# Half of an output product moved into the attention ahead of it, and a bias table fetched in two parts

## The chip, the cores and the metric

The program runs on one core of one Trainium2 chip. The metric is the device time of one execution in microseconds (us); smaller is better.

## The reference

Two transformer blocks of depth 2 act on x of 512 tokens by 1024 channels, batch 1, in float32. The change touches the second block only. There, for each of two layers:

```python
proj = x @ w_in[l]                       # hq, hf, hi, hg | nq, kc, vc, ks, vs, kw, vw, gt
o_a = hgrn2_mixer(hq, hf, hi, hg, ...)   # 4 heads of 128: a gated linear recurrence
o_b = nsa_mixer(nq, kc, vc, ks, vs, kw, vw, gt, ..., rel_bias)   # 8 heads of 64
mix = concatenate([o_a, o_b]) @ w_out[l] # 1024 x 1024
x = layer_norm(ALPHA * x + mix, ...)
ffn = (silu(x @ w_gate[l]) * (x @ w_up[l])) @ w_down[l]
x = layer_norm(ALPHA * x + ffn, ...)
```

`hgrn2_mixer` is a recurrence whose output is scaled per head by its root mean square, then by silu of a gate. `nsa_mixer` is attention of three kinds for each head (compressed keys, selected blocks, a window), each with a causal mask, a bias by distance out of `rel_bias` and a softmax of its own; the three outputs are summed with gates.

## The kernel before, in words

The channels lie on the partitions: x is `xT`, 8 chunks of 128 channels by 512 tokens. Every large product is made of three matmuls for one (`product`, lines 251 to 253): operands are split into a high and a low part, and high x high, high x low and low x high are added in a PSUM bank. Weights come through a ring of two slots of 1024 columns (512 KB each). For each slot SyncE's queue loads (`load`), ScalarE makes the high part (`hi`, line 287), GpSimd subtracts for the low part (`lo`, line 295), TensorE multiplies and counts `slots_done`. Loads, `hi` and `lo` of slot n wait for slot n-2.

All engines have their instructions in an order written out by hand, and wait for each other on counting semaphores. In the second block a layer runs:

1. Input projections, then the recurrence `pe_hgrn` / `act_hgrn` / `dve_hgrn` / `pool_hgrn`: 16 units (4 heads of 4 token chunks). Decays fill banks 0 and 1 and are read by ScalarE (`dec_exp`), scores fill banks 2 and 3 and are masked by VectorE (`a_mask`), outputs of head h gather in bank 4 + h % 2 (`ho_ready`). The last six column tiles of the projection are made in halves between the first twelve units (`pe_turn`). For each head then: ScalarE squares (line 1704), TensorE forms the mean in bank 7 (`mean_square`, line 1639), ScalarE takes the root (lines 1713 and 1717), VectorE scales (`head_out`, line 1738, semaphore `hout`), GpSimd gates and splits (`gated`, lines 1790 to 1796, three steps of `hmix` per head). For the last head this stands at the very end.
2. The three-way attention `pe_nsa` / `dve_nsa` / `act_nsa`: 16 units, four pairs of heads (hp) by four query tiles (i); unit u has (i + 1) x 128 keys. `scores(u)` (line 1855) writes six maps, VectorE adds the bias from `tab2` and takes the minimum (line 1974), ScalarE exponentiates and sums (line 2008), VectorE normalises (`post`, lines 1932 to 1945), TensorE turns the probabilities through banks 5 and 6 (`turn`, line 1865, first the selected ones SLC, then the window WIN), ScalarE copies them back (`back`, line 1992). Once per pair the compressed map is turned (`turn_cmp`, line 1874, bank 7) and copied (`back_cmp`, line 1952), and the value product `pv` (lines 1885 and 1894) fills bank 7, which `take` splits (lines 1998 and 1956, semaphore `o_taken`). `tab2`, the whole bias table of 8 heads (2 MB), lies over the recurrence's operands and is loaded when the last recurrence unit is done (line 2087).
3. The output product `pe_out`: 8 column tiles m of 8 chunks, 24 matmuls each, alternately in banks 4 and 5, one weight slot per tile; `dve_sum` (line 2022) adds ALPHA x, `add_output` sums for the norm. Its chunks 0 to 3 are the recurrence's heads, 4 to 7 the attention's pairs.
4. Layer norm, feed-forward, layer norm.

The last lines of `pe_nsa` before, which set TensorE's order:

```python
scores(0)
scores(1)
for u in range(NU):
    if u + 2 < NU:
        scores(u + 2)
    turn(u, SLC)
    if u and u % NT == 0:
        pv(u // NT - 1)
    turn(u, WIN)
    if u % NT == NT - 1:
        turn_cmp(u // NT)
pv(NSA // 2 - 1)
```

## Time and profile before

| | |
|---|---|
| median of 3 runs | 3761.97 us (3760.66 to 3763.39) |
| profiled execution | 3766.26 us, span 3764.5 us |
| TensorE busy, mean granted clock | 3539.1 us (94%), 0.969 |
| VectorE, ScalarE, GpSimd busy | 1628.5, 1251.0, 1442.9 us |
| attention of the second block, first layer | 2378.8 to 2490.0 us |
| output product, first layer | 2490.0 to 2533.9 us |

A line of a timeline has start and duration in us, engine, line of the code, operation, output <- inputs, shapes and count of merged instructions; in brackets the idle time before it and what ended it. PE is TensorE, PEld its weight load, DVE VectorE, ACT ScalarE, POOL GpSimd, SPq SyncE's queue. A line of a windows view has from:to and length in us, then busy time (and instructions) of PE, PEld, DVE, ACT and POOL, then the granted clock of TensorE (1.00 is 2.4 GHz, 0.50 is 1.2), the share of the DMA engines and GB/s. Matmuls are pipelined, so the durations of successive ones overlap: the distance of two starts is the price of one. A plain f32 matmul shows as two instructions.

### The profile page before, as it was taken

To read this page: it belongs to the slowest core of one execution; us is meant where nothing else is said; L and a number is where in the kernel's file an instruction comes from. 1 tells how busy PE (TensorE), PEld (TensorE's weight loads), DVE (VectorE), ACT (ScalarE), POOL (GpSimd) and SP (SyncE) were. 2 spreads that over 40 slices of the span, in tenths; PEclk is the share of its full clock that TensorE was granted. 3 is DMA by queue.
4 is the path that set the end of the run, shared out by engine and by line. 5 is a ranking of instruction groups with operands and counts; after the bars stand their busy time and mean duration, and the time that the engine had idled before them with its cause. 6 is when DMAs were issued, how large, how long until landed. Compare 5 with 4: busy or idle time off the path is not lost. (4 is left out here: it accounts for less than half of the span.)

```text
span 3764.5 us, 45087 instructions
## 1 busy us (share of the span) xinstructions
PE 3539.1 (94%) x16148; PEld 2780.2 (74%) x16148; DVE 1628.5 (43%) x2540; ACT 1251.0 (33%) x2114; POOL 1442.9 (38%) x615
## 2 busy tenths in 40 slices
PE   7999899899989998998999899789999898899998
PEld 5888766688868887666888687467887676568886
DVE  5441354644244423456442429634321548533312
ACT  2222346322232223464222343543222433622222
POOL 3444321344434443222444335123445244024443
PEclk9999999999999999999999999899999998899999
DMA  4223311222323223211323321012223221013222
GB/s 150 97 94 97 106 62 34 76 97 94 97 73 100 95 97 105 68 40 62 100 95 97 118 79 34 34 46 75 97 95 97 100 69 46 1 57 100 95 94 91
DMA packets 85520, 307.10 MB, mean 82 GB/s; under 512 B 11109, under 2 KB 11749, under 8 KB 83854
## 3 DMA queue, kind: packets, MB, share of 16 engines
q1 hardware_dynamic: 85390, 305.38, 24.8%
q8 instruction: 80, 1.31, 0.2%
q14 instruction: 50, 0.41, 0.0%
HBM read 301.13 MB, written 4.21 MB: 81 GB/s over the span
## 5 line engine op out<-in xcount | busy, mean ns | idle before, releaser
L295 POOL TENSOR_TENSOR wL<-ring,wH 128x1024 fp32r<-128x1024 f32 (+1 forms) x536 | 1307.9, 2440 | 2031.6 <-ACT wH L287 2031.6
L251 PE MATMUL bank<-hH,wH 128*128 128x512 f32 x2624 | 1048.1, 399 | 86.1 <-DVE hL L380 43.9
L252 PE MATMUL bank<-hL,wH 128*128 128x512 f32 x2624 | 1034.3, 394 | 0.0
L253 PE MATMUL bank<-hH,wL 128*128 128x512 f32 x2624 | 1034.1, 394 | 0.0
L287 ACT ACTIVATE wH<-ring 128x1024 fp32r<-128x1024 f32 (+1 forms) x536 | 562.9, 1050 | 1246.8 <-PE bank L253 1068.0
L251 PEld LDWEIGHTS bank<-hH,wH 128*128 128x128 f32 x2624 | 501.1, 191 | 210.8 <-issue 68.2
L253 PEld LDWEIGHTS bank<-hH,wL 128*128 128x128 f32 x2624 | 500.3, 191 | 106.6
L252 PEld LDWEIGHTS bank<-hL,wH 128*128 128x128 f32 x2624 | 501.3, 191 | 103.6 <-issue 1.4
L251 PE MATMUL bank<-guH,wH 128*128 128x512 f32 x1248 | 488.0, 391 | 2.3 <-ACT early L1088 1.4
L253 PE MATMUL bank<-guH,wL 128*128 128x512 f32 x1248 | 485.7, 389 | 0.0
L252 PE MATMUL bank<-guL,wH 128*128 128x512 f32 x1056 | 410.8, 389 | 0.0
L251 PEld LDWEIGHTS bank<-guH,wH 128*128 128x128 f32 x1248 | 234.4, 188 | 55.2 <-ACT early L1088 2.2
L253 PEld LDWEIGHTS bank<-guH,wL 128*128 128x128 f32 x1248 | 234.4, 188 | 49.2
L252 PEld LDWEIGHTS bank<-guL,wH 128*128 128x128 f32 x1056 | 198.2, 188 | 40.8
L584 DVE TENSOR_TENSOR gfull<-bank,work 128x512 f32<-128x512 f32 x88 | 60.7, 690 | 379.9 <-PE bank L253 379.9
L591 DVE CAST guH<-gfull 128x512 f32 x132 | 213.0, 1614 | 19.6 <-DVE gfull L589 4.1
L324 DVE TENSOR_TENSOR acc<-acc,work 128x512 f32<-128x512 f32 x36 | 74.8, 2078 | 287.9 <-ACT work L486 287.9
L593 DVE TENSOR_TENSOR guL<-gfull,guH 128x512 f32 x132 | 190.4, 1442 | 16.3 <-DVE guH L591 0.2
L513 ACT ACTIVATE work<-work 128x512 f32<-128x512 f32 x88 | 55.6, 632 | 422.2 <-DVE work L581 422.2
L589 DVE TENSOR_TENSOR gfull<-work,bank 128x512 f32<-128x512 f32 x44 | 30.3, 688 | 297.8 <-PE bank L253 285.0
L2022 DVE SCALAR_TENSOR_TENSOR yT<-xT,bank 128x512 f32<-128x512 f32 (+1 forms) x32 | 22.0, 687 | 276.4 <-PE bank L253 276.4
L680 PE MATMUL bank<-wH,hH 128*128 128x512 f32 (+1 forms) x320 | 120.6, 377 | 5.5 <-POOL wL L295 3.5
(236 smaller groups left out, 3774.3 us busy)
## 6 DMA issues: line engine op xcount, KB each, us to landing
ring<-in_w SPq DMA_DIRECT2D x376, 512.0 KB, 3.3
ring<-in_down SPq DMA_DIRECT2D x96, 448.0 KB, 3.2
ring<-in_down SPq DMA_DIRECT2D x48, 512.0 KB, 3.3
ring<-in_next SPq DMA_DIRECT2D x16, 512.0 KB, 3.3
mix<-in_table SPq DMA_DIRECT2D x2, 2560.0 KB
mix<-bias SPq DMA_DIRECT2D x2, 2048.0 KB
ring<-in_vg SPq DMA_DIRECT2D x8, 280.0 KB, 2.8
xT<-in_xT SPq DMA_DIRECT2D x4, 512.0 KB, 6.6
```

The lines of the kernel that those rows point to most:

```text
L251: eng.matmul(out, a, hi, start=first, stop=False)
L252: eng.matmul(out, a, lo, start=False, stop=False)
L253: return eng.matmul(out, b, hi, start=False, stop=last)
L287: eng.activation(parts_of(n, per)[0][:, 0:width], ring[:, n % NSLOT, 0:width], ACT.Copy).then_inc(w_hi, 1)
L295: eng.tensor_tensor(l[:, 0:width], ring[:, n % NSLOT, 0:width], h[:, 0:width], ALU.subtract).then_inc(w_lo, 1)
L324: eng.tensor_tensor(acc, acc, sq[:, m % 2, :], ALU.add).then_inc(sq_used, 1)
L513: eng.activation(tmp[:, k, :], src, ACT.Silu).then_inc(silu_ready, 1)
L584: eng.tensor_tensor(full, up, rs, ALU.mult).then_inc(gsteps, 1)
L589: eng.tensor_tensor(full, tmp[:, k, :], up, ALU.mult).then_inc(gsteps, 1)
L591: eng.tensor_copy(at_h, full).then_inc(gsteps, 1)
L593: eng.tensor_tensor(at_l, full, at_h, ALU.subtract).then_inc(g_free, 1)
L680: eng.matmul(out, x, a, start=(kc == 0), stop=False)
```

## The change

The output product's four recurrence chunks and its four attention chunks become two products with weight slots of their own (`split_out(..., 4)`: slot n_out2 + m // 2 holds the recurrence chunks of tiles 2k and 2k + 1, slot n_out2 + 4 + m // 2 the others).

- Recurrence half: eight tiles of 12 matmuls in bank 7, inside `pe_nsa`. Tile 0 in two parts (three heads after `scores(1)`, the last head in unit 0), tiles 1 to 7 between the two turns of units 2, 6, 7, 10, 11, 14, 15. VectorE adds ALPHA x and writes each to `early` or `early_more` (`dve_early2`, at its step u + 2, ahead of `post`).
- Attention half after `pe_nsa` (`pe_out2`), 12 matmuls a tile; VectorE adds the stored tile (`dve_out2`). ScalarE's `hi` of three weight slots moves into `act_nsa`.
- `turn_cmp` uses bank 4 in place of bank 7 and goes ahead of the unit's turns; VectorE's `back_cmp` goes ahead of the next unit's maps.
- The last head's mean square goes behind `scores(0)`, its `head_out` behind VectorE's first maps; `pe_nsa` waits for the third head's output only.
- The bias rows of heads 0 and 4 (0.5 MB) are loaded into `early[:, 6:8]` when the last projection slot is used; the other six heads' rows (1.5 MB) after the recurrence, waited for at unit 4.

The diff, without declarations and the hunks that only move a definition:

```diff
@@ -1633,9 +1637,7 @@
             def mean_square(h):
 
                 eng.wait_ge(hsq, h + 1)
-                eng.wait_ge(st_ready, min(3 * h + 6, 12))
-                if h == HG - 1:
-                    eng.wait_ge(hrs, 2 * h - 1)
+                eng.wait_ge(st_ready, 3 * h + 6)
                 eng.matmul(bank[7][:, :], onesD, sq[:, h % 2, :], start=True, stop=True).then_inc(hsum, 1)
 
             def update(u):
@@ -1679,7 +1681,12 @@
                     output(u - 1)
                 if u < 2 * LATE2:
                     pe_turn(eng, T2_EARLY + u // 2, range(4 * (u % 2), 4 * (u % 2) + 4))
-            mean_square(HG - 1)
+
+        def pe_hgrn_last(eng):
+            eng.wait_ge(hsq, HG)
+            eng.wait_ge(st_ready, 12)
+            eng.wait_ge(hrs, 2 * HG - 3)
+            eng.matmul(bank[7][:, :], onesD, sq[:, (HG - 1) % 2, :], start=True, stop=True).then_inc(hsum, 1)
 
         LATE2 = 16 - T2_EARLY
 
@@ -1716,6 +1723,13 @@
                         eng.wait_ge(hout, h)
                     eng.activation(rs, lnv, ACT.Exp, scale=-0.5).then_inc(hrs, 1)
 
+        def dve_head_out(eng, h):
+            eng.wait_ge(hrs, 2 * h + 2)
+            if h >= 2:
+                eng.wait_ge(hmix, 3 * (h - 2) + 1)
+            eng.scalar_tensor_tensor(tmp[:, h % 2, :], bank[4 + h % 2][:, :], gwcol, rs,
+                                     ALU.mult, ALU.mult).then_inc(hout, 1)
+
         def dve_hgrn(eng):
             eng.wait_ge(k_back, 4)
 
@@ -1839,8 +1845,10 @@
             return bank[2 * (w - 1) + g][:, 0:m]
 
         def pe_nsa(eng):
-            eng.wait_ge(hout, 4)
             eng.wait_ge(tp_free, 16)
+            eng.wait_ge(dec_exp, 2 * HU)
+            eng.wait_ge(a_mask, A_MASKS * HU)
+            eng.wait_ge(hout, HG - 1)
 
             def scores(u):
                 hp, i = divmod(u, NT)
@@ -1868,15 +1876,14 @@
 
             def turn_cmp(hp):
                 eng.wait_ge(c_norm, 4 * hp + 4)
-                if hp:
-                    eng.wait_ge(o_taken, hp)
                 for m in range(2):
-                    mm = eng.transpose(bank[7][:, m * P:(m + 1) * P], pslot_c[:, hp % 2, m, :], ident)
+                    mm = eng.transpose(bank[4][:, (2 + m) * P:(3 + m) * P], pslot_c[:, hp % 2, m, :], ident)
                 mm.then_inc(c_turn, 1)
 
             def pv(hp):
                 eng.wait_ge(p_back, 16 * (hp + 1))
                 eng.wait_ge(c_back, hp + 1)
+                eng.wait_ge(early_out, EARLY_BEFORE[hp])
                 o = bank[7]
                 for w in range(2):
                     for j in range(NT):
@@ -1897,17 +1904,69 @@
                 mm.then_inc(o_ready, 1)
 
             scores(0)
+            pe_hgrn_last(eng)
             scores(1)
+            pe_early2(eng, 0, (0, 1, 2))
+            eng.wait_ge(hout, HG)
             for u in range(NU):
                 if u + 2 < NU:
                     scores(u + 2)
+                if u % NT == NT - 1:
+                    turn_cmp(u // NT)
                 turn(u, SLC)
                 if u and u % NT == 0:
                     pv(u // NT - 1)
+                if u == 0:
+                    pe_early2(eng, 0, (3,))
+                if u in EARLY2_AT:
+                    pe_early2(eng, EARLY2_AT.index(u) + 1)
                 turn(u, WIN)
-                if u % NT == NT - 1:
-                    turn_cmp(u // NT)
             pv(NSA // 2 - 1)
+
+        EARLY2_AT = (2, 6, 7, 10, 11, 14, 15)
+        EARLY_BEFORE = [1 + sum(u < 4 * (hp + 1) for u in EARLY2_AT) for hp in range(NSA // 2)]
+        A2 = B2 = 4
+        A2_MADE = [(hmix, 3 * h + 3) for h in range(HG)]
+        B2_MADE = [(o_taken, 1 + hp) for hp in range(NSA // 2)]
+
+        def early2(m):
+
+            return early[:, m, :] if m < 4 else early_more[:, m - 4, :]
+
+        def pe_early2(eng, m, qs=None):
+
+            if m and (qs is None or qs[0] == 0):
+                eng.wait_ge(early_out, m)
+            elif qs[0] == 0:
+                eng.wait_ge(hrs, 2 * HG - 1)
+            for k, hp in enumerate(range(3)):
+                if m == 1 + sum(u < 4 * (hp + 1) for u in EARLY2_AT):
+                    eng.wait_ge(o_taken, hp + 1)
+            pe_tile(eng, bank[7][:, :], n_out2, A2, m, A2_MADE, [guH[:, HQ + h, :] for h in range(HG)],
+                    [guH[:, HGT + h, :] for h in range(HG)], qs)
+
+        def dve_early2(eng, m):
+
+            eng.wait_ge(*tile_end(n_out2, A2, m, 0))
+            eng.scalar_tensor_tensor(early2(m), xT[:, m, :], ALPHA, bank[7][:, :],
+                                     ALU.mult, ALU.add).then_inc(early_out, 1)
+
+        def pe_out2(eng):
+
+            n1 = n_out2 + A2
+            h, l = ([v[:, kc, :] for kc in range(HG, KD)] for v in (hH, hL))
+            first = (0, 1, 2)
+            for m, qs in ((0, first), (1, first), (0, (3,)), (1, (3,))) + tuple((m, None) for m in range(2, KD)):
+                if qs is None:
+                    eng.wait_ge(y_done, m + 1)
+                pe_tile(eng, bank[4 + m % 2][:, :], n1, B2, m, B2_MADE, h, l, qs)
+
+        def dve_out2(eng, m):
+
+            if m == 0:
+                eng.wait_ge(early_out, KD)
+            eng.wait_ge(*tile_end(n_out2 + A2, B2, m, KD // 2))
+            eng.tensor_tensor(yT[:, m, :], bank[4 + m % 2][:, :], early2(m), ALU.add).then_inc(y_done, 1)
 
         def dve_gates(eng):
             eng.wait_ge(gate_ready, 1)
@@ -1921,7 +1980,8 @@
             eng.wait_ge(p_rec, 3)
 
         def dve_nsa(eng):
-            eng.wait_ge(tab_in, 16)
+            eng.wait_ge(tab_first, 16)
+            eng.wait_ge(ho_ready, HU)
             eng.memset(pslot_c[:, :, :, :], 0.0).then_inc(c_zero, 1)
             eng.wait_ge(c_zero, 1)
 
@@ -1949,7 +2009,7 @@
                 eng.wait_ge(c_turn, hp + 1)
                 if hp >= 2:
                     eng.wait_ge(o_ready, hp - 1)
-                eng.tensor_copy(probC[:, hp % 2, 0:2 * P], bank[7][:, 0:2 * P]).then_inc(c_back, 1)
+                eng.tensor_copy(probC[:, hp % 2, 0:2 * P], bank[4][:, 2 * P:4 * P]).then_inc(c_back, 1)
 
             def take(hp):
                 eng.wait_ge(o_hi, hp + 1)
@@ -1960,10 +2020,14 @@
                     hp, i = divmod(u, NT)
                     n, r = (i + 1) * P, u % 3
                     c0 = S - P - i * P + CMP_END
+                    if u >= 5 and i == 1:
+                        back_cmp(hp - 1)
+                    if u == NT:
+                        eng.wait_ge(tab_rest, 32)
                     for o, (w, g) in enumerate(READ):
-                        h = hp + 4 * g
+                        table = tab2[:, hp + 4 * g, :] if hp else early[:, 6 + g, :]
                         m = cw(i) if w == CMP else n
-                        bias = tab2[:, h, c0:c0 + 16 * (m - 1) + 1:16] if w == CMP else tab2[:, h, S - n:S]
+                        bias = table[:, c0:c0 + 16 * (m - 1) + 1:16] if w == CMP else table[:, S - n:S]
                         out = cmp_slot(u, g) if w == CMP else pslot[r][:, w - 1, g, 0:m]
                         eng.wait_ge(s_ready, 6 * u + WRITTEN[o])
                         if w == CMP:
@@ -1973,8 +2037,14 @@
                             eng.wait_ge(p_turn, 4 * (u - 3) + 2 * (w - 1) + g + 1)
                         eng.tensor_tensor_reduce(out, score_bank(w, g, m), bias, 1.0, 3.0e38,
                                                  ALU.add, ALU.min, least[r][:, 3 * g + w:3 * g + w + 1]).then_inc(p_max, 1)
-                if u >= 5 and (u - 1) % NT == 0:
-                    back_cmp((u - 1) // NT - 1)
+                if u == NU + 1:
+                    back_cmp(NSA // 2 - 1)
+                if u == 0:
+                    dve_head_out(eng, HG - 1)
+                if u == 2:
+                    dve_early2(eng, 0)
+                if u - 2 in EARLY2_AT:
+                    dve_early2(eng, EARLY2_AT.index(u - 2) + 1)
                 if 1 <= u <= NU:
                     post(u - 1)
                 if u >= 6 and (u - 2) % NT == 0:
@@ -2011,6 +2081,8 @@
                     take((u - 1) // NT - 1)
                 if 1 <= u <= NU:
                     back(u - 1)
+                if u in (4, 9, 13):
+                    hi(eng, n_out2 + 2 + (4, 9, 13).index(u))
 
 
         def dve_sum(eng, q, n1, per_tile, m, i=0, per=0):
@@ -2082,9 +2154,12 @@
                     for k, c in enumerate(VG_ROWS):
                         load(sp, n_vg + k, t["vg_2"][bass.ds(layer, 1), k, :, 0:c * VG].rearrange("a p n -> (a p) n"), c * VG)
                     stream(sp, layer, t["w8_2"], 18, 8, n_in2 + 22, WIDE)
+                    sp.wait_ge(slots_done, n_out2)
+                    sp.wait_ge(bias_out, 16)
+                    sp.dma_start(early[:, 6:8, :], t["bias"][:, 0:NSA:4, :]).then_inc(tab_first, 16)
                     sp.wait_ge(ho_ready, HU)
-                    sp.wait_ge(bias_out, 16)
-                    sp.dma_start(tab2, t["bias"]).then_inc(tab_in, 16)
+                    for h in (1, 5):
+                        sp.dma_start(tab2[:, h:h + 3, :], t["bias"][:, h:h + 3, :]).then_inc(tab_rest, 16)
                     stream(sp, layer, t["w8_2"], 26, KD - 2 + A, n_out2 + 2, WIDE)
                     stream_down(sp, layer, t["down_2"], 0, n_ffn2 + A)
                     stream(sp, layer, t["next_2"], 0, 4, n_next2, WIDE)
@@ -2111,10 +2186,7 @@
                     pe.wait_ge(vp_free, 12)
                     pe_hgrn(pe)
                     pe_nsa(pe)
-                    pe_out(pe, n_out2, ln_free(0), [(hmix, 12), None, None, None]
-                           + [(o_taken, 1 + pair) for pair in range(4)],
-                           [guH[:, HQ + h, :] for h in range(HG)] + [hH[:, kc, :] for kc in range(HG, KD)],
-                           [guH[:, HGT + h, :] for h in range(HG)] + [hL[:, kc, :] for kc in range(HG, KD)])
+                    pe_out2(pe)
                     pe_layer_norm(pe, 0)
                     pe_ffn(pe, 0, n_ffn2, 8, ln_free(1))
                     pe_layer_norm(pe, 1)
@@ -2151,8 +2223,7 @@
                     act.activation(gate, vg[:, :, 256:280], ACT.Exp, scale=-1.0).then_inc(gate_ready, 1)
                     act_hgrn(act)
                     act_nsa(act)
-                    for m in range(KD):
-                        hi(act, n_out2 + m + 2)
+                    act_hi(act, n_out2 + 5, 5)
                     act_ln(act, 0)
                     act_split(act, 0, None, False)
                     act_silu(act, 0, n_ffn2)
@@ -2178,7 +2249,7 @@
                     dve_hgrn(dve)
                     dve_nsa(dve)
                     for m in range(KD):
-                        dve_sum(dve, 0, n_out2, 1, m)
+                        dve_out2(dve, m)
                         add_output(dve, 0, m)
                     dve_ln(dve, 0, g1, b1, 8)
                     dve_ffn(dve, 0, n_ffn2, False)
@@ -2358,7 +2429,7 @@
         hq, hf, hi, hg, nq, kc, vc, ks, vs, kw, vw, gt = (w_in_2[l][:, c[i]:c[i + 1]] for i in range(12))
         w8 += [columns(np.concatenate([kc, vc, hq[:, :P]], 1)), rows(hf, 512, 2),
                columns(np.concatenate([hq[:, P:], hg], 1)), rows(hi, 512, 2),
-               columns(np.concatenate([ks, kw, nq[:, order]], 1)), columns(np.concatenate([w_out_2[l][:512], w_out_2[l][512:][order]])),
+               columns(np.concatenate([ks, kw, nq[:, order]], 1)), split_out(np.concatenate([w_out_2[l][:512], w_out_2[l][512:][order]]), 4),
                gate_up(w_ffn_gate_2[l], w_ffn_up_2[l])]
         vg.append(parts(np.concatenate([vs, vw, gt], 1).reshape(KD, P, VG), VG_ROWS, VG))
         w11.append(down(w_ffn_down_2[l]))
```

## Rows read from the trace of the kernel before

**Rows 1.** The page's first line: the span.

```profile
span 3764.5 us, 45087 instructions
```

**Rows 2.** Windows: starts of both attentions, three pairs, and parts of pairs.

```profile
2378.80:2396.40 17.60, 14.38 (x55) 9.14 (x56) 10.74 (x62) 8.72 (x40) 3.13 (x3) 0.50 0.29 121
2396.40:2484.20 87.80, 70.54 (x452) 44.30 (x450) 51.84 (x251) 61.68 (x219) 0.00 (x0) 0.90 0.00 1
...
3187.90:3198.40 10.50, 7.29 (x36) 5.68 (x36) 5.45 (x39) 4.76 (x24) 3.13 (x3) 0.50 0.48 201
...
2411.20:2436.20 25.00, 20.57 (x141) 12.99 (x140) 15.58 (x80) 17.53 (x67) 0.00 (x0) 0.93 0.01 2
...
2462.50:2484.20 21.70, 15.70 (x102) 9.68 (x101) 10.90 (x43) 13.67 (x45) 0.00 (x0) 0.92 0.00 1
...
3219.00:3247.40 28.40, 24.68 (x140) 15.17 (x138) 15.88 (x81) 18.18 (x67) 0.00 (x0) 0.76 0.01 1
...
3272.40:3295.20 22.80, 17.72 (x101) 10.78 (x100) 10.89 (x43) 13.65 (x45) 0.00 (x0) 0.78 0.00 0
```

**Rows 3.** Timeline, first layer, from the last projection to the second scores.

```profile
2346.81 0.39 PE L253 MATMUL bank<-hH,wL 128*128 128x512 f32 x1
...
2374.28 0.39 PE L1665 MATMUL bank<-yT,mix 128*128 128x128 f32 x2
...
2374.70 0.33 SPq L2087 DMA_DIRECT2D mix<-bias  x1
...
2375.35 1.34 PE L1639 MATMUL bank<-work,mats 128*128 128x512 f32 x2 [0.69 <-ACT work L1704]
...
2378.82 1.87 PE L1855 MATMUL bank<-mix 64*128 64x7 f32 x12 [2.13 <-DVE work L1738]
...
2382.60 0.48 DVE L1925 MEMSET mix<- 128x512 f32 x1 [3.83 <-DMA mix<-bias]
...
2383.65 6.17 PE L1855 MATMUL bank<-mix 64*128 64x15 f32 x24 [2.95 <-DVE mix L1974]
```

**Rows 4.** Timeline of TensorE, first layer, inside the attention.

```profile
2402.15 0.89 PE L1865 MATMUL bank<-mats,mix 128*128 128x128 f32 x6 [2.37 <-ACT mix L1992]
2402.97 2.62 PE L1855 MATMUL bank<-mix 64*128 64x15 f32 x12
...
2411.21 0.64 PE L1885 MATMUL bank<-mix 128*64 128x512 f32 x1
...
2432.51 1.12 PE L1865 MATMUL bank<-mats,mix 128*128 128x128 f32 x8 [0.34 <-ACT mix L1992]
...
2433.77 2.11 PE L1855 MATMUL bank<-mix 64*128 64x23 f32 x12
...
2478.50 4.04 PE L1865 MATMUL bank<-mats,mix 128*128 128x128 f32 x18 [3.06 <-ACT mix L1992]
...
2484.20 0.61 PE L1885 MATMUL bank<-mix 128*64 128x512 f32 x1 [0.61 <-DVE mix L1952]
```

**Rows 5.** Timeline of TensorE, second layer: recurrence's end, first and last value product.

```profile
3183.31 0.39 PE L1665 MATMUL bank<-yT,mix 128*128 128x128 f32 x2
...
3219.05 0.64 PE L1885 MATMUL bank<-mix 128*64 128x512 f32 x1
...
3295.57 0.61 PE L1885 MATMUL bank<-mix 128*64 128x512 f32 x1 [0.61 <-DVE mix L1952]
```

**Rows 6.** Timeline, first layer: the output product's first matmul and its end.

```profile
2489.96 0.50 PE L251 MATMUL bank<-guH,wH 128*128 128x512 f32 x1
...
2533.83 0.69 DVE L2022 SCALAR_TENSOR_TENSOR yT<-xT,bank 128x512 f32<-128x512 f32 x1 [4.03 <-PE bank L253]
2533.89 1.06 ACT L287 ACTIVATE wH<-ring 128x1024 fp32r<-128x1024 f32 x1 [4.38 <-PE bank L253]
...
2535.02 2.42 POOL L295 TENSOR_TENSOR wL<-ring,wH 128x1024 fp32r<-128x1024 f32 x1 [2.97 <-ACT wH L287]
```

**Rows 7.** The source view of line 591: count, then shortest, median and longest duration.

```profile
L591 DVE CAST guH<-gfull x132: 426/2371/2395, 51.8 to 3607.0; 128x512 f32 x132
```

13 lines of the change are left out of this document (5 added, 8 removed).

## Prediction

> **What bounds the kernel now.** I read the page first: the span is 3764.5 us and the profiled execution took 3766.3 us, so 1.8 us lie around the span; the median of the runs, 3762.0, is 4.3 us below it [rows 1]. Durations below are of the profiled execution; the difference that they give is taken from the median. Within 0.2% (7.5 us) is what a measurement of this kernel can't tell from no change.
>
> Then the windows of the second block's three-way attention, once per layer: from 2378.8 us in the first layer, from 3187.9 in the second, four head pairs of four units each [rows 2]. In the 87.8 us from 2396.4 to 2484.2 TensorE is busy for 70.5, ScalarE for 61.7, VectorE for 51.8. No engine is full; TensorE is nearest. The granted clock is 0.50 for the first 17.6 us (10.5 in the second layer), 0.90 after. Only 1.2 and 2.4 GHz are granted; 0.90 is a mixture.
>
> Last the timelines. At the start [rows 3] TensorE ends the recurrence at 2374.67 (2374.28 + 0.39), then the last head's mean square, two ScalarE steps and a VectorE step pass before the first scores at 2378.82, and VectorE's memset waits for the 2 MB table (issued 2374.70) until 2382.60. Inside a pair [rows 4] the longest hole of TensorE is 2.37 us, between the two turns (transposes) of the third unit; the scores behind it take 2.62 us against 2.11 for the next unit's, which have more columns: both run 12 instructions, so the clock fell in the hole. Another hole, before the fourth unit's second turn, is only 0.34 us. A pair lasts 25.0 us at best [rows 2]. The output product behind it is solid TensorE work: 192 matmuls from 2489.96 to 2533.83, 0.2285 us apiece [rows 6].
>
> **The change part by part.**
>
> *Output product, removed part.* Half the matmuls, 96 in a layer, leave the stage after the attention: 96 x 0.2285 = 21.9 us a layer. What is left starts at once: six chunks (18 matmuls, 4.1 us) need only the first three pairs, so the last pair's split, two steps of VectorE and ScalarE of about 0.65 us each, stays hidden. Its four weight slots: the second is converted by ScalarE (1.06 us) and GpSimd (2.42 us, [rows 6]) right behind the attention, ready at about +4.1 us and needed at +5.5; the third is ready at +9.2 and needed at +11. So no new wait. VectorE's add per tile has the price of the fused one that it replaces, once per 2.74 us: hidden.
>
> *The same matmuls, added inside.* Eight tiles of 12 matmuls, 2.74 us each, so that nothing is saved that TensorE can't take into its holes. Tile 0 falls in the start (below). Of the other seven, four are behind a third unit's first turn, in the 2.37 us hole: 2.74 - 2.37 = +0.4 each. Three are behind a fourth unit's first turn, where the hole is 0.34: +2.4 each. Queued behind a tile on TensorE is the second turn, for which ScalarE's copy waits, and with it the pair's value product.
>
> VectorE reads each tile out (0.69 us) in its own order, ahead of the normalisation of the unit. At units 4, 8, 12 it reaches that point about 1.5 us before the tile is ready and waits; TensorE has scores and a turn to do in that time, so I take no cost (bounds: nothing, and 1.5 + 0.69 three times a layer, if TensorE ran out).
>
> ScalarE converts three weight slots inside (1.06 us each). The first falls before ScalarE's wait for a value product: free. The other two come at its fullest, and some 0.7 us each shows. GpSimd subtracts three (2.42 each). In the feed-forward stages, where GpSimd subtracts all along, a VectorE cast of 128x512 has a median of 2371 ns against 426 ns for the shortest [rows 7]; so the bounds are nothing and 3 x 2.4 = 7.3 us a layer. At the places in question VectorE is mostly at operations that read PSUM, so I take 1 us a layer; the upper bound is 12.6 us more over both.
> The Trainium skill (SBUF — State Buffer, Who interferes with whom) has the rule: VectorE and GpSimd share a port pair, the first one holds it for its instruction, and tensor_scalar, which does the normalisation here, is among the operations that can need it. The median of the cast agrees. It speaks against the change: by it, with every subtraction met, 3732 us.
>
> *Clock inside.* The two pairs whose windows have a clock of 0.93 and 0.76 last 25.0 and 28.4 us [rows 2]: 1.75 and 6.8 us of clock lost, 3.4 us between them, so 0.67 us of time per us lost. At full clock a pair would be about 23.8, and the last pair (21.7 at 0.92, 23.2 at 0.78, [rows 2, 5]) about 21.0. Against the pairs with the better clocks that is 1.2 + 1.2 + 0.7 = 3.1 us; with the long hole filled, I give the change half of it. Then the three pairs after the first value product take:
> second 23.8 + 0.4 + 2.4 = 26.6; third 26.6 + 0.7 = 27.3; last, where the first tile lies in a hole of 3.06 us [rows 4] and is free, and the second delays the final value product by about 1.8 (2.74 less some 0.9 of small holes): 21.0 + 0.7 + 1.8 = 23.5. Together 77.4, plus 1.6 for the half of the clock not regained: 79.0. Before: 72.99 in the first layer (2411.21 to 2484.20), 76.52 in the second (3219.05 to 3295.57). So +6.0 and +2.5 us.
>
> *The start.* The first pair's table (0.5 MB) is asked for when the last projection is done, about 2347 and so 27 us early [rows 3]; the other 1.5 MB are needed only at unit 4. At the rate of before (2 MB in 7.9 us) they take 6 us: hidden. The queue had nothing else to issue there, and the next weights follow as now. VectorE can start at 2374.7. TensorE does: scores 0 at once, then the mean square, scores 1, nine matmuls of tile 0. With scores 0 ahead of the mean square, the two ScalarE steps end near 2379.2, and the exponentials can follow; now they wait for a map behind the memset, past 2383.1. TensorE is then the longest chain. Its work up to the first value product, at full clock: 0.95 + 1.0 + 1.3 + 2.1 (nine matmuls) + 2.1 for scores 0, mean square, scores 1, tile, scores 2, then 0.4 + 0.7 + 0.7 + 2.5 for the turn, the last three matmuls, the turn, scores 3, and some 14.8 for the turns of units 1 to 4, scores 4 to 6, tile 1 and two short holes: 26.5, less 1 for rows that overlap, 25.5. Half clock costs half its length. Before, the work behind scores 0 stayed at 1.2 GHz from 2383.65 to 2396.4 (12.7 us) in one layer, and in the other for 5.4 us of work (7.3 busy less 1.9 for scores 0) [rows 2, 3]. I take 9 us: +4.5, and 1 us for first waits: 31.0. Before: 2411.21 - 2374.67 = 36.5, and 3219.05 - 3183.70 (3183.31 + 0.39) = 35.3 [rows 3 to 5]. So -5.5 and -4.3 (bounds by the two lengths: 1.9 either way).
>
> **Sum.** First layer -5.5 + 6.0 + 1.0 - 21.9 = -20.4; second -4.3 + 2.5 + 1.0 - 21.9 = -22.7. Together -43 us: 3766.3 becomes 3723, and the median of runs 3762 - 43 = 3719 us.
>
> **The rivals.**
> A. *The attention is full: the tiles are only moved.* For: TensorE's rows leave 17 us of 88 idle, and some of that is latency. Then each of seven tiles shows whole, 19.2 us, and only the start pays. Per layer -21.9 + 19.2 - 5 + 1 + 1.4 = -5: 3752 us. Against: the hole of 2.37 us is a wait for ScalarE, and a tile needs no ScalarE.
> B. *The clock stays at 2.4 GHz* because TensorE no longer stops. Then 1.6 us per layer come back, the start costs 4.5 less, and with GpSimd's meetings nil it is 7.1 more per layer: 3705 us. For: the clock falls only after holes. Against: at 2375 TensorE has just had the thin end of the recurrence, and the clock was down by 2378.8 [rows 2].
> The Trainium skill (TensorE: Matmul & The Clock Gate, Part 1) says that activity releases the throttle and idleness restores it, at two levels only; the rows agree with both levels. It is what B would rest on.
> C. *The table was hidden anyway*, or the start is bound by TensorE at half clock throughout: the start gives nothing, and the sum is -43 + 10: 3729 us. In range; against it stands the 5 us between 2378.82 and 2383.65 in which TensorE did 1.87 us of work.
> D. *Slower: the tile readout in VectorE's queue becomes the chain.* Each of seven tiles at half clock is 12 x 0.457 = 5.5 us, plus 0.69 read out before the unit's normalisation, so 6.2 us late for the next turn: 43 us, against 21.9 + 5 saved. +16 per layer: 3794 us. It decides once a tile costs over 3.8 us. Against: TensorE has 2 us of scores between a tile and the turn that needs the normalisation, and the clock inside a pair is mostly full.
>
> **How the numbers follow.** Forecast with C and partial clocks 0.72, A 0.10, B 0.14, D 0.04. The predicted time is 3719. The range goes down to 3706 (most of B) and up by the unknown costs: port meetings 12.6 of which half, the start 4, no clock regained 3, one more exposed tile: 3736. Faster 0.94 (A too), same 0.03, slower 0.03.
>
> **What the profile after would show.** The output stage after the attention at about 22 us, with no hole between its slots. The first VectorE map at some 0.5 to 1 us behind the recurrence's last matmul. Value product to value product 26.6 and 27.3. No hole of 2.37 us. The fourth unit's tile followed by the second turn with hardly a wait. What would make me wrong: ScalarE's back copies late by more than the tiles (pairs over 29 us), normalisations that stretch to 2 us beside GpSimd, a half clock that outlives 2388, or a hole in the short output product because a weight slot isn't split in time.

## The result, and the profile after

The changed kernel takes 3716.07 us (median of 4 runs, 3713.38 to 3719.51) beside 3762.68 us (3760.66 to 3768.27) for the kernel before on the same chip: a ratio of 0.9875, 95% interval 0.9860 to 0.9891. That is 46.6 us less; 3719 was predicted. The profiled executions differ by more, 3766.26 to 3713.38 or 52.9 us, because the one of before lies 3.6 us above its median and the one of after 2.7 us below. The two stages that were changed give 51.0 of the 52.9.

First the page's first line after (3764.5 in [rows 1]), and the windows after: in each layer from the recurrence's last matmul to the first value product, then value product to value product three times, then (first layer) the last value product and the output product.

```profile
span 3711.6 us, 45111 instructions
```

```profile
2375.35:2404.54 29.19, 27.86 (x154) 18.29 (x154) 23.50 (x121) 22.50 (x85) 6.97 (x7) 0.88 0.26 91
2404.54:2430.42 25.88, 24.15 (x163) 16.14 (x163) 16.41 (x81) 18.24 (x71) 1.71 (x1) 1.00 0.07 21
2430.42:2457.55 27.13, 25.71 (x164) 16.98 (x163) 16.68 (x81) 18.42 (x67) 2.36 (x1) 0.94 0.07 21
2457.55:2481.76 24.21, 21.21 (x125) 13.49 (x124) 11.68 (x41) 14.79 (x46) 2.36 (x1) 0.93 0.07 22
2481.76:2487.53 5.77, 5.70 (x49) 2.95 (x49) 0.00 (x0) 0.00 (x0) 0.00 (x0) 1.00 0.01 3
2487.53:2510.10 22.57, 22.36 (x98) 17.86 (x96) 10.27 (x15) 4.73 (x5) 10.28 (x4) 1.00 0.24 75
3156.76:3184.94 28.18, 26.52 (x154) 17.49 (x155) 23.33 (x121) 22.50 (x85) 6.96 (x7) 0.94 0.27 95
3184.94:3212.05 27.11, 25.69 (x164) 17.10 (x163) 16.52 (x81) 18.38 (x71) 1.70 (x1) 0.94 0.06 20
3212.05:3239.16 27.11, 25.69 (x164) 16.94 (x163) 16.66 (x81) 18.41 (x67) 2.36 (x1) 0.94 0.06 21
3239.16:3263.35 24.19, 21.26 (x126) 13.47 (x125) 11.73 (x41) 14.80 (x46) 2.36 (x1) 0.93 0.07 22
```

The lengths say where the time went. The "start" is the first window of a layer, the "pairs" are the next three, the "output" is the last value product and the output product:

| us | before | after | change | predicted |
|---|---|---|---|---|
| start, layer 1 | 36.54 | 29.19 | -7.35 | -5.5 |
| pairs, layer 1 | 72.99 | 77.22 | +4.2 | +6.0 |
| output, layer 1 | 49.63 | 28.34 | -21.3 | -21.9, +1.0 ports |
| start, layer 2 | 35.35 | 28.18 | -7.17 | -4.3 |
| pairs, layer 2 | 76.52 | 78.41 | +1.9 | +2.5 |
| output, layer 2 | 49.66 | 28.34 | -21.3 | -21.9, +1.0 ports |

(Output before: 2484.20 to 2533.83 in [rows 4, 6].) Pairs that took 25.0 to 28.4 us before [rows 2] now hold two tiles, 5.5 us of TensorE work, and take 25.9 to 27.1. The first pair after has a clock of 1.00; the others have 0.93 or 0.94.

The start is the least steady of these. In a second profiled execution of the changed kernel ("changed once more" below) the two starts take 30.70 and 29.18 us in place of 29.19 and 28.18, so their gain there is 5.8 and 6.2 us; of the kernel before there is one profile only.

The timeline of the start after, to be held against [rows 3]:

```profile
2347.71 0.64 SPq L2159 DMA_DIRECT2D early<-bias  x1
...
2374.96 0.39 PE L1667 MATMUL bank<-yT,mix 128*128 128x128 f32 x2
2375.38 1.14 PE L1863 MATMUL bank<-mix 64*128 64x7 f32 x12
2376.11 0.29 DVE L2038 CUSTOM_DVE_ANT_0 mix<-bank,early 128x128 f32<-128x128 f32 x1
2376.46 2.07 PE L1689 MATMUL bank<-work,mats 128*128 128x512 f32 x2
2378.46 2.83 PE L1863 MATMUL bank<-mix 64*128 64x15 f32 x12
2379.74 0.39 ACT L2078 ACTIVATE mix<-mix 128x128 f32<-128x128 f32 x1
2381.22 0.79 PE L254 MATMUL bank<-guH,wH 128*128 128x512 f32 x1
```

The first map of VectorE starts 0.76 us behind the recurrence, where before it stood behind the memset of 2382.60; scores, mean square, scores and tile follow each other on TensorE without a wait. Two windows show the half clock, which ends by about 2383 and not at 2396.4 as before [rows 2]:

```profile
2377.00:2383.00 6.00, 6.00 (x18) 3.38 (x17) 3.29 (x20) 4.40 (x21) 3.69 (x5) 0.50 0.98 363
2383.00:2387.00 4.00, 4.00 (x22) 2.47 (x22) 3.35 (x13) 1.72 (x9) 1.03 (x1) 0.98 0.21 85
```

TensorE's timeline inside the first two pairs, beside [rows 4]:

```profile
2411.34 0.47 PE L1873 MATMUL bank<-mats,mix 128*128 128x128 f32 x2 [0.96 <-ACT mix L2062]
2411.74 2.54 PE L1863 MATMUL bank<-mix 64*128 64x31 f32 x12
...
2417.95 0.48 PE L254 MATMUL bank<-guH,wH 128*128 128x512 f32 x1
...
2420.79 0.82 PE L1873 MATMUL bank<-mats,mix 128*128 128x128 f32 x6
...
2427.05 1.03 PE L1873 MATMUL bank<-mats,mix 128*128 128x128 f32 x8
...
2437.22 0.47 PE L1873 MATMUL bank<-mats,mix 128*128 128x128 f32 x2 [0.96 <-ACT mix L2062]
2437.62 4.07 PE L1863 MATMUL bank<-mix 64*128 64x31 f32 x12
2441.62 0.66 PE L1873 MATMUL bank<-mats,mix 128*128 128x128 f32 x4
2442.63 0.68 PE L1873 MATMUL bank<-mats,mix 128*128 128x128 f32 x4 [0.35 <-ACT mix L2062]
```

The tile of the third unit starts at 2417.95 and the window turn follows at 2420.79 with no wait: the hole of 2.37 us is gone. So is the wait ahead of the fourth unit's second turn (2427.05). What is left is the hole of 0.96 us behind a value product, and a dip of the clock behind it: the same twelve matmuls take 2.54 us behind the first value product and 4.07 behind the second. A dip stands behind five of the six value products that have a pair following.

### The profile page after: what moved, and what is told of

The parts are those of the page before. It is cut to its first block and busy times, and to the rows that moved or that the text cites. A ratio compares the mean times of both kernels' runs of the same rounds, so it can differ in the third digit from the quotient of the medians.

```text
span 3711.6 us, 45111 instructions
## 1 busy us (share of the span) xinstructions
PE 3515.2 (95%) x16148; PEld 2758.6 (74%) x16148; DVE 1640.3 (44%) x2556; ACT 1249.8 (34%) x2114; POOL 1444.4 (39%) x615
## 3 DMA queue, kind: packets, MB, share of 16 engines
q1 hardware_dynamic: 86222, 305.38, 24.8%
## 5 line engine op out<-in xcount | busy, mean ns | idle before, releaser
L685 PE MATMUL bank<-wH,hL 128*128 128x512 f32 (+1 forms) x320 | 119.2, 373 | 0.0
```

The source lines that it names most:

```text
L685: mm = eng.matmul(out, y, a, start=False, stop=(kc == KD - 1))
```

## The experiments

"Before" and "changed" are the two kernels. All ran with the kernel before on the same chip; a gain is the ratio's.

| run | median us | ratio to before (95%) |
|---|---|---|
| the start alone | 3757.33 | 0.9981 (0.9972 to 0.9991) |
| the tiles alone | 3728.92 | 0.9902 (0.9888 to 0.9916) |
| first table late | 3721.59 | 0.9884 (0.9870 to 0.9898) |
| before, idle work in third units | 3746.80 | 0.9958 (0.9945 to 0.9971) |
| before, idle work in fourth units | 3778.33 | 1.0046 (1.0033 to 1.0060) |
| changed, scores moved up | 3737.37 | 0.9928 (0.9915 to 0.9942) |
| changed, readout behind | 3714.44 | 0.9877 (0.9862 to 0.9892) |
| changed, tiles in second units | 3716.87 | 0.9880 (0.9865 to 0.9895) |
| changed, ScalarE's take later | 3717.28 | 0.9868 (0.9852 to 0.9885) |
| changed, idle work behind value product | 3718.92 | 0.9875 (0.9858 to 0.9891) |
| changed once more | 3719.99 | 0.9880 (0.9864 to 0.9897) |
| changed, take later and idle work | 3723.76 | 0.9889 (0.9873 to 0.9906) |

**The start alone.** The output product stays whole, behind the attention; the start is the changed one, and so is the place of the compressed turn at the end of a pair (`turn_cmp`, `back_cmp`).

```diff
 scores(0)
 pe_hgrn_last(eng)
 scores(1)
-pe_early2(eng, 0, (0, 1, 2))
 eng.wait_ge(hout, HG)
...
-if u in EARLY2_AT:
-    pe_early2(eng, EARLY2_AT.index(u) + 1)
...
-pe_out2(pe)
+pe_out(pe, n_out2, ...)
```

> The start of the change without its tiles: table of the first pair early, the last head's mean square behind scores 0, turn_cmp in bank 4; the output product as before. Theory (my sum: the start is a term of its own, worth 5.5 and 4.3 us with tile 0 in it, so some 9 us a layer without tile 0's nine matmuls at half clock): 3762 - 18 = about 3744 us. Rival C (the table was hidden anyway, or TensorE at half clock bounds the start): within 5 us of before, 3757 to 3762.

The kernel gains 7 us by the ratio (3 to 11 by its interval), not the 18 of my theory. That is near the 5 that rival C allowed, but not for its reason. The starts do get shorter, 30.35 and 28.87 us, so 6.2 and 6.5 less than before. But the first layer's three pairs take 27.44, 27.38 and 22.71 us, 4.5 more than before; the second layer's take the same as before in all. The hole of 2.37 us and the slow work behind it are still in each third unit, as they were before. What is new in the first layer stands elsewhere, behind the hole of 0.96 us that follows a value product: there the five microseconds have a clock of 0.66 in all three pairs here, and before in the second pair only. The first pair, before and here:

```profile
2418.01:2423.01 5.00, 4.36 (x26) 2.50 (x26) 3.77 (x17) 4.36 (x19) 0.00 (x0) 1.00 0.01 2
2410.30:2415.30 5.00, 5.00 (x18) 2.55 (x18) 2.75 (x12) 3.50 (x16) 0.00 (x0) 0.66 0.00 0
```

The gain of the start is real; in the first layer of this profile the pairs gave most of it back. Beside the tiles the start is worth more: the whole change less the tiles alone (next run) is 10 us.

**The tiles alone.** The whole table is fetched behind the recurrence and the last head is finished ahead of scores 0, as before; the output product is split. TensorE's order and the queue's:

```diff
+pe_hgrn_last(eng)
+eng.wait_ge(hout, HG)
 scores(0)
-pe_hgrn_last(eng)
 scores(1)
 pe_early2(eng, 0, (0, 1, 2))
-eng.wait_ge(hout, HG)
...
+sp.wait_ge(ho_ready, HU)
 sp.wait_ge(bias_out, 16)
-sp.dma_start(early[:, 6:8, :], t["bias"][:, 0:NSA:4, :]).then_inc(tab_first, 16)
-sp.wait_ge(ho_ready, HU)
-for h in (1, 5):
-    sp.dma_start(tab2[:, h:h + 3, :], t["bias"][:, h:h + 3, :]).then_inc(tab_rest, 16)
+sp.dma_start(tab2, t["bias"]).then_inc(tab_in, 16)
```

> The tiles of the change without its start: the whole table in one transfer after the recurrence and the last head's mean square and scaling ahead of scores 0, as before; all eight tiles inside the attention. Theory (tiles take holes and keep the clock up): product -21.3 a layer, pairs +4.2 and +1.9 as the trace after shows, tile 0 some +3.4 a layer since it stands after scores 1: 3762 - 29 = about 3733 us, and with the start alone it adds up to the whole. Rival A (only moved): -21.3 + 19.2 + 3 a layer: 3764 us.

The tiles gain 37 us by themselves, where my theory gave 29. Rival A (only moved) is out. The starts take 35.3 and 35.7 us with tile 0 in them, as long as before: that tile lies free in the wait for the table. The pairs are those of the changed kernel (25.86, 27.14, 24.09). With the start's 7 us the sum is 44, near the 46.6 of the whole.

**First table late.** Only the early fetch is undone; the order of the start stays.

```diff
-sp.wait_ge(slots_done, n_out2)
+sp.wait_ge(ho_ready, HU)
 sp.wait_ge(bias_out, 16)
 sp.dma_start(early[:, 6:8, :], t["bias"][:, 0:NSA:4, :]).then_inc(tab_first, 16)
-sp.wait_ge(ho_ready, HU)
```

> The kernel after with one thing undone: the first pair's 0.5 MB are asked for when the recurrence has ended, ahead of the other 1.5 MB. Theory (the order of the last head is what the start gains, since ScalarE's exponentials can't begin before its root at 2379.7, 3.6 us behind the first map): a late table of 0.5 MB lands some 3 us after the recurrence, map at +3.5 to +4 instead of +0.8, exponentials 0 to 1 us later: 3716 to 3719 us. Rival (the early fetch is the start's gain): 4 to 5 us a layer given back, 3725 us.

I expected almost nothing, and in the profile that fell. The starts are 32.73 and 32.62 us, 3.5 and 4.4 more than in the changed kernel's first profile, 2.0 and 3.4 more than in its second. The ratio moves by 0.0009 only, some 3 us, and the two intervals overlap, so the times alone can't tell my theory from the rival; the price is taken from the profiles. Its timeline:

```profile
2374.34 0.64 SPq L2159 DMA_DIRECT2D early<-bias  x1
2374.34 1.13 PE L1863 MATMUL bank<-mix 64*128 64x7 f32 x12
2375.03 1.05 SPq L2161 DMA_DIRECT2D mix<-bias  x2
...
2379.72 0.48 DVE L1985 MEMSET mix<- 128x512 f32 x1 [5.52 <-DMA early<-bias]
...
2380.76 2.83 PE L1863 MATMUL bank<-mix 64*128 64x15 f32 x12 [3.54 <-DVE mix L2038]
```

0.5 MB asked for at 2374.34 hold VectorE up until 2379.72, 5.4 us, where the whole 2 MB had taken 7.9. The other 1.5 MB are asked for 0.7 us behind it and weights 2.2 us behind it. In the 5.4 us the queue moves 192 GB/s, which is 1.0 MB, twice the first transfer: so the later transfers share that time, and a quarter of the data doesn't come in a quarter of the time. About half of the start's gain is the early fetch (5.5 of 12.0 us over both layers against the one profile of the changed kernel, 7.9 of 14.5 against the other), the other half the new order.

**Idle work in the third units.** The kernel before, with twelve matmuls whose result nobody reads in the long hole.

```diff
 turn(u, SLC)
 if u and u % NT == 0:
     pv(u // NT - 1)
+if u % NT == 2:
+    filler(u // NT)     # 12 matmuls of 128x512 into bank 7
 turn(u, WIN)
```

> The kernel before with 12 more matmuls of 128x512 (a tile's 2.74 us) between the two turns of each pair's third unit, their result thrown away; nothing else changed. Clock theory (the 2.37 us hole drops the clock, filling it keeps 2.4 GHz): 0.4 us a pair added, 1 to 1.5 us a pair regained: 3754 to 3759 us, attention windows at a clock of 0.95 or more. Rival (only occupancy counts): + 0.4 x 8 = 3765 us, clock as before.

The kernel becomes 0.42% faster, some 16 to 19 us, by doing more: 2.0 to 2.4 us for each of eight fillings. Three pairs of it, one with a dip and two without:

```profile
2407.80:2432.93 25.13, 23.04 (x151) 14.90 (x150) 15.42 (x79) 17.43 (x67) 0.00 (x0) 0.93 0.01 2
2432.93:2456.95 24.02, 21.64 (x151) 13.92 (x151) 15.37 (x79) 17.26 (x67) 0.00 (x0) 1.00 0.01 1
3207.76:3231.78 24.02, 21.64 (x152) 13.91 (x151) 15.36 (x79) 17.26 (x67) 0.00 (x0) 1.00 0.01 2
```

A pair with a full clock and its long hole filled takes 24.02 us, where before 25.0 was the best and 28.4 the worst [rows 2]. It does more work and is 1.0 to 4.4 us shorter, and its clock is 1.00 in place of 0.93 to 0.76: the difference was the clock's. So a tile in a third unit costs less than nothing. Part of this lies behind the value products: a dip stands there in one of six places here, in three of six before. Whether the filling took those two away or chance did isn't shown.

**Idle work in the fourth units.** The same matmuls, placed where the hole is 0.34 us.

```diff
-if u % NT == 2:
+if u % NT == 3 and u < NU - 1:
     filler(u // NT)
```

> The kernel before, with the same twelve thrown-away matmuls of 128x512 into bank 7 as in the run with idle work in the third units, but now behind the fourth unit's first turn of the first three pairs (six times in all). It prices the term '+2.4 us for a tile in the fourth unit'. My term (occupancy: the hole there is 0.34 us, so a tile shows 2.4): six times 2.4, 14 us slower than before, about 3778 beside 3764. Rival (the clock pays there too, as it did in the third units): the tile removes 1 to 2 us of half clock per pair, and the time is within 4 us of before, 3760 to 3768.

It is 16 to 17 us slower (by medians and by ratio), 2.7 to 2.9 for each of six; the interval of the ratio gives 2.1 to 3.8, so my 2.4 holds and the rival (within 4 us of before) is out. One pair has nearly the clock that it had before, the second of the second layer: 27.15 us at 0.94 here, 24.97 there, +2.2. The three other filled pairs that can be compared take 3.7, 3.8 and 0.0 us more, at other clocks.

```profile
3252.71:3279.86 27.15, 23.06 (x151) 15.06 (x150) 15.58 (x80) 17.51 (x67) 0.00 (x0) 0.94 0.00 1
```

**Scores moved up.** In the changed kernel, scores(u + 3) right behind the value product.

```diff
-if u + 2 < NU:
+if u + 2 < NU and not (u > 1 and u % NT == 1):
     scores(u + 2)
...
     pv(u // NT - 1)
+    scores(u + 3)
```

> The changed kernel, with the scores that follow each of the first three value products of a layer moved up to stand right behind it, ahead of the window turn for which TensorE waits 0.96 us there. Theory (that hole is what lowers the clock: the scores behind it take 4.1 us instead of 2.5 in five of six pairs): the hole of 0.96 is filled and the dip of 1.5 us goes, in five or six pairs 1.2 to 2.4 us each: 7 to 12 us faster than the changed kernel's 3716, so 3704 to 3709. Rival (ScalarE is the fuller engine behind a value product, with the copy of its high part and the back copies, and TensorE's order sets its supply): the window turn comes 2.5 us later, the back copies with it, and the time is 0 to 15 us slower, 3716 to 3731.

It is some 20 us slower than the changed kernel, more than the rival gave. TensorE behind the value product:

```profile
2410.67 2.54 PE L1863 MATMUL bank<-mix 64*128 64x31 f32 x12
2413.14 0.44 PE L1873 MATMUL bank<-mats,mix 128*128 128x128 f32 x2
2413.93 0.63 PE L1873 MATMUL bank<-mats,mix 128*128 128x128 f32 x4 [0.35 <-ACT mix L2063]
2417.33 0.68 PE L1873 MATMUL bank<-mats,mix 128*128 128x128 f32 x4 [2.78 <-ACT mix L2063]
...
2420.41 0.77 PE L254 MATMUL bank<-guH,wH 128*128 128x512 f32 x1
```

The hole isn't filled but moved: ScalarE gets its turned tiles 2.5 us later, returns them later, and TensorE waits 2.78 us two turns on. Behind that hole the clock has fallen: 0.70 from 2417.33 to 2423.00, and the first tile matmul takes 0.77 us in place of 0.48. Behind the value product itself there is no dip in any of the six places, now that the scores stand there in place of the hole. That gains nothing here.

**Readout behind the normalisation, and tiles in the second units.** Two moves within the changed kernel, one run each.

```diff
-if u - 2 in EARLY2_AT:
-    dve_early2(eng, EARLY2_AT.index(u - 2) + 1)
 if 1 <= u <= NU:
     post(u - 1)
+if u - 2 in EARLY2_AT:
+    dve_early2(eng, EARLY2_AT.index(u - 2) + 1)
```

The second of the two:

```diff
-EARLY2_AT = (2, 6, 7, 10, 11, 14, 15)
+EARLY2_AT = (2, 5, 6, 9, 10, 13, 14)
```

> The changed kernel, with each tile's readout in VectorE's order behind the unit's normalisation instead of ahead of it. It prices the mechanism of rival D (the readout stands in the chain), which the prediction put at nothing. Theory: VectorE's waits of 1.5 to 2.4 us for a tile lie inside slack, so the normalisation coming earlier gives nothing: 3716, within 4 us. Rival: the readout does hold up the turn: each of the seven tiles gives back 0.7 to 2.2 us, 10 to 30 us faster, 3686 to 3706.

> The changed kernel, with the three tiles of the fourth units moved to the second units of the next pairs' order (units 5, 9, 13 in place of 7, 11, 15), where TensorE's wait between the turns is 0.66 us instead of 0.3 to 0.5. Theory (occupancy decides, a tile costs 2.7 less the hole wherever it stands): each costs about 0.2 to 0.3 less, 3714 beside 3716, not to be told apart. Rival (the place matters to the clock: the second unit has the fewest columns behind the hole that follows a value product, so work added there keeps the clock up): 1 us for each pair, 3708 to 3711.

3714.4 and 3716.9 us: both as the changed kernel. VectorE's waits for a tile (2.43 us and 1.53 us in the first pair after) cost nothing that these runs can tell, where rival D would have given back 10 to 30 us. Three tiles a layer may stand in second or in fourth units: pairs of 25.8 and 27.3 us in place of 25.9 and 27.1.

**The dip behind the value product.** What is left of clock loss stands behind the hole of 0.96 us. Three edits, and the changed kernel again as their neighbour.

```diff
 # take later (ScalarE)
-if u >= 5 and (u - 1) % NT == 0:
-    take((u - 1) // NT - 1)
 if 1 <= u <= NU:
     back(u - 1)
+if u >= 5 and (u - 1) % NT == 0:
+    take((u - 1) // NT - 1)
```

```diff
 # idle work (TensorE), 8 transposes, or 3 together with the take later
     pv(u // NT - 1)
+    eng.wait_ge(p_max, 6 * (u + 3))
+    for k in range(8):
+        eng.transpose(bank[4][:, (2 + k % 2) * P:(3 + k % 2) * P], pslot_c[:, (u // NT - 1) % 2, k % 2, :], ident)
```

> The changed kernel, with one change of order on ScalarE: behind a value product it first copies the turned probabilities of the next unit back and only then takes the high part of the value product (0.60 us). The window turn of TensorE waits for those copies: its hole of 0.96 us behind each of six value products becomes about 0.35. Theory (that hole lowers the clock: the scores behind it take 4.1 us instead of 2.5 in five of six pairs): 0.6 us six times and some of the five dips of 1.2 us, 4 to 10 us faster than the changed kernel: 3706 to 3712, and pairs of 25.3 to 26.5. Rival (the clock falls there whatever the hole, and ScalarE sets the next turn): within 3 us of it, 3713 to 3719, with the 4.1 us scores still there.

> The changed kernel, with eight thrown-away transposes of 128x128 (some 0.85 us, into the half of bank 4 that is free there) behind each of the first three value products of a layer, inside the hole of 0.96 us. They add work and move nothing. Theory (the hole lowers the clock): the scores behind it take 2.5 us in all pairs, all pairs last some 25.9, five dips of 1.2 us go: 3709 to 3711 beside the changed kernel's 3716. Rival (the hole is not the cause, only the thin matmuls of the value product's end are, or chance): 3715 to 3719.

> The changed kernel once more, unchanged, on the same chip as the two above, since they are told from it by a few us. Both theories: ratio to the kernel before 0.9875, 3714 to 3718, pairs of 25.9 (no dip) or 27.1 (dip behind the value product).

> The changed kernel with both: ScalarE takes the value product behind the back copies, and three thrown-away transposes fill the 0.35 us that are left of the hole. Theory (clock): no dip in any pair, pairs of 25.3, 10 to 12 us faster than the changed kernel, 3704 to 3707. Rival (dips stay whatever the hole): as the take alone, 3712 to 3719.

None can be told from the changed kernel, let alone beats it: the medians lie at 3717 to 3724 with it at 3720, and all ratios' intervals overlap. By the time alone the rivals hold. The profiles say more. With the take later, the hole is 0.53 us in all six places and the dip still stands in four; in the two others, the third pairs, TensorE waits 2.08 us one unit on, where it waits 0.35 us in the changed kernel. With idle work the hole is gone, and the scores behind it take 2.54 us in all six pairs, in both kernels that have it. So the theory was right that work in the hole stops that dip. It was wrong about what that is worth. The second pair with eight transposes, TensorE and then ScalarE:

```profile
2431.42 1.09 PE L1921 MATMUL bank<-mats,mix 128*128 128x128 f32 x8
2432.44 0.47 PE L1873 MATMUL bank<-mats,mix 128*128 128x128 f32 x2
2432.84 2.54 PE L1863 MATMUL bank<-mix 64*128 64x31 f32 x12
2435.31 0.66 PE L1873 MATMUL bank<-mats,mix 128*128 128x128 f32 x4
2437.56 0.87 PE L1873 MATMUL bank<-mats,mix 128*128 128x128 f32 x4 [1.59 <-ACT mix L2065]
2438.36 1.97 PE L1863 MATMUL bank<-mix 64*128 64x7 f32 x12
```

```profile
2432.95 0.27 ACT L2065 ACTIVATE yT<-bank 128x128 f32<-128x128 f32 x1
2433.12 1.05 ACT L290 ACTIVATE wH<-ring 128x1024 fp32r<-128x1024 f32 x1
2434.07 0.61 ACT L2081 ACTIVATE mix<-mix 128x384 f32<-128x384 f32 x1
...
2437.05 0.36 ACT L2065 ACTIVATE mix<-bank 128x256 f32<-128x256 f32 x1
```

```profile
2438.36:2444.00 5.64, 5.64 (x25) 4.73 (x25) 2.18 (x15) 4.58 (x16) 0.00 (x0) 0.50 0.18 68
```

TensorE, now quick, waits 1.59 us for ScalarE's back copy at 2437.05, which stands behind a weight conversion of 1.05 us (line 290) and the exponentials. Behind that hole the clock is 0.50 for 5.6 us, into the next tile. The pair takes 29.83 us in place of 27.13. The first pairs, which have no conversion there, take 25.87 and 25.88 in the two layers, where the changed kernel had 25.88 and 27.11 in one profile and 27.10 and 25.87 in the other: there the filling does pay, some 1.2 us in one layer of two. Over both layers the pairs take 162.0 us, 6.4 more than in the changed kernel. The time shows less of that than 6.4 us. The starts of this profile, which the edit leaves alone, are 1.4 and 3.9 us shorter than in the two profiles of the changed kernel; the rest isn't traced. A version with the two conversions one unit earlier, ahead of ScalarE's wait for the value product, together with the filling, follows from this; it was not tried.

The hole of 0.96 us is the same in the kernel before, with and without idle work, and in the changed ones, but what follows it is not. Counted over the six places of each profile, a dip (a clock of 0.66 or less over the 5 us behind the hole) stands in 3 in the kernel before, in 1 with idle work in third units, in 2 with it in fourth units; in 5 with the start alone, in 5 and 5 in the changed kernel, in 5 with the readout behind, in 4 with the tiles alone, the table late or the tiles in second units. Behind the second and third value products of a layer it stands in all 28 places of the last seven profiles and in 3 of 12 of the first three. The start alone and the tiles alone have in common, against the kernel before, the compressed turn moved ahead of the last unit's turns (`turn_cmp` in bank 4, with `back_cmp` ahead of the maps). So that move is the suspect for these dips. No run makes it alone, and it stays open.

## Why the prediction was right, step by step

**Output product, -21.9 a layer: right, -21.3 measured.** 43.87 us became 22.57. 96 matmuls at 0.2285 are 21.9; the other 0.6 are seams, 0.17 of it one wait for VectorE's add. No weight slot was late: ScalarE converts at 2488.14 and GpSimd's 2.40 us from 2489.27 end at 2491.7, before the 2493 at which I had it needed.

**Third unit's tile, +0.4: right for occupancy.** The filled pair takes 24.02 us at a full clock; I had worked out 23.8 without the tile.

**Fourth unit's tile, +2.4: right, or slightly too high.** A pair after with a full clock takes 25.88, which is 24.02 + 1.9. The profile with idle work in third units shows why: with the long hole filled, the hole ahead of the fourth unit's second turn has grown from 0.34 to 0.67 us, and 2.74 less 0.67 is 2.1. The six idle fillings at that place cost 2.7 to 2.9 each (2.1 to 3.8 by the interval); in that kernel the long hole is still open, and the filling that I looked at behind a third unit's half clock took 3.68 us where another took 3.00.

**ScalarE's conversions, +0.7 each: hidden, and for a reason that I had not seen.** The second pair of the second layer holds one and takes 27.11 us; the first pair there holds none and takes the same. In both the clock dips behind the value product for 1.5 us, and ScalarE does the conversion meanwhile. Take the dip away and the conversion shows: the hole grows from 0.65 to 1.59 us, by 0.94.

**Ports, +1.0 a layer: nothing in the time.** VectorE's normalisation of 128x512 has a mean of 480 ns after, 16 of them in the first layer's attention. GpSimd's three subtractions for the weights (2.36 us each, from 2403.87, 2439.03 and 2466.15) meet VectorE only in its maps, which read PSUM and one tile of SBUF, and these keep their 0.69 us (mean 689 ns for 128x512).
A meeting did take place, where I hadn't looked for it. The changed order puts GpSimd's subtraction for the last head beside the first unit's normalisations, of 128x128. The four together take 1.91 us, and 0.87 before (line L1945), where nothing stood beside them:

```profile
2382.72 1.31 POOL L1802 TENSOR_TENSOR guH<-mix,guH 128x512 fp32r<-128x512 f32 x1
2382.79 1.91 DVE L2005 TENSOR_SCALAR mix<-mix 128x128 f32<-128x128 f32 x4
2387.40 0.87 DVE L1945 TENSOR_SCALAR mix<-mix 128x128 f32<-128x128 f32 x4
```

The first of the four takes 1325 ns where the others take 274 to 276, and ends at 2384.11, just behind the subtraction (2384.03). In the second layer the four take 1.90 us beside the same subtraction. The time doesn't show it: TensorE has the scores of the third unit to do until 2386.4.
The Trainium skill (SBUF — State Buffer, Who interferes with whom) speaks of instructions that need the shared port, tensor_scalar among them; these normalisations agree with it, and none of those in the pairs met a subtraction.

**Clock inside: right in kind, and the remaining loss under-sized.** I gave 1.6 us a layer for what would not come back. Measured are two dips in the first layer and three in the second, 1.25 us each (27.13 or 27.11 less 25.88): 2.5 and 3.7. I also had them in the wrong place, behind the long hole; they stand behind the one of 0.96 us. That 25.88 is less than my 26.6 made up for it, which is luck: 77.2 and 78.4 in all, against 79.0. The experiment with idle work shows that occupancy alone did not set the pairs before: with more work in them they got shorter, at a higher clock.
By the Trainium skill (TensorE: Matmul & The Clock Gate, Part 1), a gate lowers the clock according to how busy the array is; pairs that get shorter when idle matmuls are added agree with it.

**The start, -5.5 and -4.3: too small by 1.9 and 2.9 in the profiled execution.** Of these 4.7 us, 2.5 are that execution's: with the starts of the changed kernel's second profile, -5.8 and -6.2, the first layer's term is right within 0.4 and the second's too small by 1.9. The term that was mis-sized is "I take 9 us" of half clock. The windows after have a mean clock of 0.88 and 0.94; a mixture of 1.00 and 0.50, that is 7.0 us of half clock in 29.19 and 3.4 in 28.18. At half the length the 2.0 and 5.6 us less make 1.0 of the 1.9 and 2.8 of the 2.9. The second profile has 0.83 and 0.88, so 10.4 and 7.0 us. What is left of each miss, 0.9 us at most, lies in the work at full clock: I added up 25.5, and the windows less the loss at half clock and less TensorE's idle time (1.3 and 1.7 us) leave 24.4 and 24.8, an estimate. Of the start's gain, about half is the early table, as the late one shows. Rival C (nothing there) is out by the windows of the start in every profile that has it, and by the whole less the tiles alone, 10 us, though the start on its own is worth only 7 us: its first layer's pairs came out 4.5 us longer, with a dip behind each value product.

**The sum.** -20.4 and -22.7 were predicted, -24.4 and -26.6 measured in the profiles, 7.9 us more: 4.7 from the start (2.5 of them the execution's), 2.4 from the pairs, 2.0 from the ports, less 1.2 for the seams of the output product. The medians show 46.6 where the profiles show 52.9, so the forecast of 43 was missed by less in the runs, 3.6 us, than in the profiles. The two profiled executions lie on opposite sides of their medians, as worked out above.

**The rivals.** A is out by the tiles alone. B (the clock stays up) holds in one pair of six only. D is out by the readout moved behind, which changes nothing that can be told.

## What to carry to other kernels

If the same instructions take longer behind a hole than elsewhere, work moved into that hole can pay twice: it is gone from where it stood, and the clock behind the hole comes back. Filling pays only while the engine that TensorE waits for has time left; where it hasn't, the wait comes back a turn later and longer (2.78 us behind the moved scores, 1.59 us beside a conversion). A first part split off a transfer comes early only if it is also asked for early: asked for together with the rest, a quarter of the table took 5.4 us of the whole table's 7.9.

## What the runs showed that I had not expected

Doing useless work made the kernel before 0.42% faster. A dip of 1.5 us behind a hole of 0.96 us was free where ScalarE had a conversion to do meanwhile: with the dip taken away those pairs took 29.83 us in place of 27.1. Whether the clock dips behind one and the same hole varies: of the six value products of the changed kernel that have a pair following, five had a dip in either of its two profiled executions, but not the same five. What decides it in a given place stays open, though the same hole had fewer dips in the kernels whose compressed turn stood where it was; in both kernels whose hole was wholly filled it never stood there. One normalisation waited a microsecond for a subtraction of GpSimd, in a place that the change itself had made. And a quarter of a table, asked for just ahead of the other three, needed two thirds of the time that the whole had needed.
